# Scan of a hybrid transformer block: decay exponents as whole products with strictly triangular matrices, rows on ScalarE, weights on VectorE, prepared during the rotation

## The reference, cut to what matters

```
a_cum = jnp.cumsum(dt_c * a, axis=2)                       # within a chunk of 128 tokens
seg = a_cum[:, :, :, None, :] - a_cum[:, :, None, :, :]    # i minus j, per head
decay = jnp.exp(jnp.where(lower, seg, -jnp.inf))
scores = jnp.einsum('bcihn,bcjhn->bcijh', c_c, b_c) * decay * dt_c[:, :, None, :, :]
y_diag = jnp.einsum('bcijh,bcjhp->bcihp', scores, x_c)
y_off = jnp.einsum('bcihn,bchpn,bcih->bcihp', c_c, h_in, jnp.exp(a_cum))
```

## Time and profile before

| | us |
|---|---|
| median of 3 runs (lowest, highest) | 1417.57 (1416.66, 1420.8) |
| span of the profiled execution | 1417.9 |
| TensorE busy | 1172.4 (83%) |
| VectorE busy | 463.5 (33%) |
| ScalarE busy | 266.9 (19%) |
| GpSimd busy | 122.1 (9%) |

### The profile page before, as it was taken

The page is one execution under the profiler, slowest core; times in us unless marked ns, Lnnn a source line. Parts: engine busy times, 40 slices in busy tenths (PEclk is TensorE's granted clock), DMA queues, the critical chain, the costliest instruction groups (busy, mean ns, idle before and its releaser), DMA issues.

```text
span 1417.9 us, 15930 instructions
## 1 busy us (share of the span) xinstructions
PE 1172.4 (83%) x6032; PEld 567.1 (40%) x6032; DVE 463.5 (33%) x1121; ACT 266.9 (19%) x592; POOL 122.1 (9%) x107
## 2 busy tenths in 40 slices
PE   5899978878989599999985499986799699995553
PEld 2363433444654333333332447432468333332222
DVE  5111456764742611111101421357663511110003
ACT  1220101223530411111101322001251311110002
POOL 2000031820000010000000200033200100000001
PEclk9999999979899799999998699997689799997776
DMA  9622106739996389999999401006003689999972
GB/s 337 242 86 93 60 0 261 289 131 412 374 353 274 140 326 372 389 390 395 395 399 397 187 4 56 0 0 237 0 1 119 252 313 385 388 410 413 407 327 93
DMA packets 86997, 344.03 MB, mean 243 GB/s; under 512 B 6918, under 2 KB 42187, under 8 KB 64395
## 3 DMA queue, kind: packets, MB, share of 16 engines
q1 hardware_dynamic: 67728, 309.68, 56.5%
q10 hardware_dynamic: 15195, 19.86, 4.1%
q0 software_dynamic: 4000, 13.49, 2.7%
HBM read 300.92 MB, written 42.07 MB: 242 GB/s over the span
## 4 chain that ended last, share of the span: by engine, by line
PE 61%; DMA 20%; DVE 11%; ACT 3%; issue 2%; SPq 1%; POOL 1%; ACTq 0%; POOLq 0%; DVEq 0%
PE ps L901 13%; PE ps L503 12%; DMA ring<-in_exp_w_up 10%; PE ps L924 6%; PE ps L791 6%; PE ps L512 5%; PE ps L446 4%; DMA ring<-in_w_mod 3%; DMA slots<-arena 2%; PE ps L468 2%; DMA arena<-in_exp_w_up 2%; PE ps L688 2%; PE ps L770 2%; PE ps L668 2%; PE ps L740 1%
## 5 line engine op out<-in xcount | busy, mean ns | idle before, releaser
L901 PE MATMUL ps<-ring,arena 128*32 128x256 f32 (+1 forms) x1344 | 197.8, 534 | 45.1 <-DMA ring<-in_exp_w_up 45.1
L503 PE MATMUL ps<-u,ring 128*128 128x512 f32 (+1 forms) x416 | 168.0, 564 | 9.5 <-ACT u L1743 4.0
L446 PE MATMUL ps<-cst,arena 128*128 128x128 f32 x558 | 110.3, 318 | 65.7 <-DVE arena L1445 33.0
L446 PEld LDWEIGHTS ps<-cst,arena 128*128 128x128 f32 x558 | 70.2, 160 | 172.0 <-issue 81.5
L901 PEld LDWEIGHTS ps<-ring,arena 128*32 128x32 f32 (+1 forms) x1344 | 71.3, 136 | 154.4 <-issue 146.5
L1601 DVE TENSOR_TENSOR arena<-arena,ps 128x128 f32<-128x128 f32 (+1 forms) x59 | 27.3, 503 | 317.3 <-ACT arena L1903 317.3
L503 PEld LDWEIGHTS ps<-u,ring 128*128 128x128 f32 x416 | 80.0, 194 | 94.9 <-issue 90.1
L901 PE MATMUL ps<-arena 128*64 128x512 f32 (+1 forms) x544 | 82.2, 528 | 17.6 <-DMA arena<-in_exp_w_up 17.6
L924 PE MATMUL ps<-arena 128*32 128x256 f32 (+1 forms) x672 | 94.4, 485 | 1.6 <-ACT arena L1912 1.6
L791 PE MATMUL ps<-u,ring 128*128 128x512 f32 (+1 forms) x256 | 83.6, 487 | 2.3 <-DVE h L1426 1.3
L512 PE MATMUL ps<-ring,u 128*128 128x256 f32 (+1 forms) x224 | 76.6, 502 | 7.7 <-DVE arena L1245 7.7
(11 more groups left out here) (291 smaller groups left out, 1221.9 us busy)
## 6 DMA issues: line engine op xcount, KB each, us to landing
ring<-in_w_mod SPq DMA_DIRECT2D x24, 2048.0 KB, 10.9
ring<-in_exp_w_gate SPq DMA_DIRECT2D x22, 2048.0 KB, 18.6
ring<-in_exp_w_up SPq DMA_DIRECT2D x22, 2048.0 KB, 23.0
arena<-in_exp_w_down SPq DMA_DIRECT2D x22, 2048.0 KB, 20.1
slots<-zeros SPq DMA_DIRECT2D x4, 6144.0 KB, 41.9
arena<-in_exp_w_gate SPq DMA_DIRECT2D x10, 2048.0 KB, 20.7
u<-in_exp_w_down SPq DMA_DIRECT2D x10, 2048.0 KB, 19.7
arena<-in_exp_w_up SPq DMA_DIRECT2D x10, 2048.0 KB, 26.7
```

The costliest lines, as they stand in the source:

```text
L446: return nc.tensor.transpose(dst, src, ident[0:n, 0:n])
L503: last = nc.tensor.matmul(bank[row:row + width, 0:T - c0], w[:, k, n:n + width], u[:, k, c0:T], start=(k == 0), stop=(k == KT - 1))
L901: last = nc.tensor.matmul(ps[n * part:n * part + n, 2 + b % 2, 0:2 * width].rearrange("p (s n) -> p s n", s=2), x_k, pair[:, :, a:a + widt ...
```

## The change

Column i of head h of `rows` keeps its content, but the matrix that it is multiplied with is now strictly triangular. With M the strict triangle, (M^T rows) at (j, i) is the sum of dt*a over the tokens k with j < k <= i (forwards), which is the whole exponent. Where j is not before i the sum is empty and gives 0. So the subtraction of the sum at j and the clamp are gone, and ScalarE's exp reads the two PSUM banks itself. The masked scores, which are 0 outside the triangle, stay. The two strict matrices are made by VectorE at the end of `latents_up`, in each layer, into ground of `wuq`.

Placement: `rows` are made by ScalarE, eight instructions each, instead of one on GpSimd. `weights` is one 128x1024 product on VectorE instead of two of 128x512 on GpSimd. For tile 0 the scores, both casts, both exponentials and both weights stand in the rotation; for tile 1 the scores, casts and exponentials do, and its weights come in the scan. In the scan both casts of tile i+2 are made after the y sums of tile i. The modulation parts of layer 0 move behind the y sums (one, then two); their number is the same.

```
-SCAN_MODS = (1, 1, 1)
+SCAN_MODS = ((1, 2), (0, 0))
+        strict = [wuq[:, 0, P * d:P * d + P] for d in range(2)]
 TensorE, rotate(l):
+                masked_products(l, 0)
+                cast_rows(l, 0, 0)
                 for m in range(4):
-                    if m == 2 and l == 0:
-                        project_z(l, TT - 1)
+                    if m == 2:
+                        cast_rows(l, 0, 1)
+                        if l == 0:
+                            project_z(l, TT - 1)
...
                     spare(1)
+                masked_products(l, 1)
+                for d in range(2):
+                    cast_rows(l, 1, d)
                 read_back(f"kr{l}")
 cast_rows:
+                if n == 0:
+                    pe.wait_ge(S("to_end_ready"), l + 1)
                 pe.wait_ge(S("rows_built"), 2 * tiles_before(l) + n + 1)
                 if n >= 1:
-                    pe.wait_ge(S("decay_clamped"), 2 * tiles_before(l) + n)
+                    pe.wait_ge(S("decay_exp"), 2 * tiles_before(l) + n)
                 for b in range(2):
-                    last = nc.tensor.matmul(ps[:, 2 + b, :], ones[:, :],
+                    last = nc.tensor.matmul(ps[:, 2 + b, :], strict[d],
 TensorE, scan_tiles(l), after the y sums of tile i:
                     if i + 1 < len(tiles):
-                        cast_rows(i + 1, 1)
-                        spare(SCAN_MODS[1])
+                        spare(SCAN_MODS[l][0])
                     if i + 2 < len(tiles):
-                        scores(i + 2)
-                        cast_rows(i + 2, 0)
-                        spare(SCAN_MODS[2])
+                        masked_products(l, i + 2)
+                        cast_rows(l, i + 2, 0)
+                        spare(SCAN_MODS[l][1])
+                        cast_rows(l, i + 2, 1)
 VectorE, latents_up(l), at its end:
+                for d in range(2):
+                    link(tt(strict[d], tri[1 - d], ident, ALU.subtract))
 VectorE, rotate(l):
+                masked_scores(l, 0)
                 for m in range(4):
...
+                weights(l, 0, 0)
                 for hh in range(DA_H):
...
+                masked_scores(l, 1)
+                weights(l, 0, 1)
 VectorE:
+            def weights(l, i, d):
+                dve.wait_ge(S("decay_exp"), 2 * tiles_before(l) + 2 * i + d + 1)
+                own_read()
+                part = ews[i % 2][d].rearrange("p (g h) i -> p g h i", g=2)
+                tt(part, part, gms[i % 2][:, d].unsqueeze(2).to_broadcast([P, 2, 4, P]), ALU.mult).then_inc(
+                    S("w_ready"), 1)
 VectorE, scan_tiles(l):
                     if i + 1 < len(tiles):
-                        clamp(i + 1, 1)
+                        for d in range(2):
+                            weights(l, i + 1, d)
 ScalarE, scan(l):
+                def rows(i, d):
+                    at_dt = 32 * d + 8 * (FIRST_T[l] + i)
+                    for hh in range(SSD_H):
+                        last = a(ews[i % 2][d][:, hh, :], tri[d], ACT.Identity, scale=sc[:, 2, at_dt + hh:at_dt + hh + 1])
+                    last.then_inc(S("rows_built"), 1)
+
+                def decays(i, d):
+                    act.wait_ge(S("rows_cast"), 2 * tiles_before(l) + 2 * i + d + 1)
+                    a(ews[i % 2][d], ps[:, 2:4, :].rearrange("p b (h i) -> p (b h) i", i=P), ACT.Exp).then_inc(
+                        S("decay_exp"), 1)
+
+                act.wait_ge(S("to_end_ready"), l + 1)
+                for d in range(2):
+                    rows(0, d)
+                for d in range(2):
+                    decays(0, d)
                 wait_evac(f"z{l}{TT - 1}")
+                for d in range(2):
+                    rows(1, d)
                 a(z[:, FIRST_T[l]:TT, :], z[:, FIRST_T[l]:TT, :], ACT.Silu).then_inc(S("z_ready"), 1)
                 exp_and_ln()
+                for d in range(2):
+                    decays(1, d)
                 for i in range(n):
-                    if i + 1 < n:
-                        decays(i + 1, 1)
+                    if i + 2 < n:
+                        act.wait_ge(S("y_summed"), tiles_before(l) + i + 1)
+                        for d in range(2):
+                            rows(i + 2, d)
                     act.wait_ge(S("y_gated"), tiles_before(l) + i + 1)
...
                     if i + 2 < n:
-                        decays(i + 2, 0)
+                        for d in range(2):
+                            decays(i + 2, d)
```

More of the change, by code:

```diff
@@ L649, in scan_states, with masked_products, cast_rows @@
                         project_z(l, z_after(l, n))
+            def masked_products(l, i):
+                t = FIRST_T[l] + i
+                for g in range(2):
+                    bank = open_bank(f"cb{l}{t}{g}")
+                    r = slice(64 * g, 64 * g + 64)
+                    close_bank(nc.tensor.matmul(bank[:, 0:P], xbc[r, 4, P * t:P * t + P],
+                                                xbc[r, 5, P * t:P * t + P], start=True, stop=True))
+            def cast_rows(l, i, d):
+                n = 2 * i + d
+                if n == 0:
+                    pe.wait_ge(S("to_end_ready"), l + 1)
+                pe.wait_ge(S("rows_built"), 2 * tiles_before(l) + n + 1)
+                if n >= 1:
+                    pe.wait_ge(S("decay_exp"), 2 * tiles_before(l) + n)
+                for b in range(2):
+                    last = nc.tensor.matmul(ps[:, 2 + b, :], strict[d],
+                                            ews[i % 2][d][:, 4 * b:4 * b + 4, :].rearrange("p h i -> p (h i)"),
+                                            start=True, stop=True)
+                last.then_inc(S("rows_cast"), 1)
@@ L673, in scan_tiles @@
-                scores(0)
-                for d in range(2):
-                    cast_rows(0, d)
-                    spare(SCAN_MODS[0])
-                scores(1)
-                cast_rows(1, 0)
                 for i, t in enumerate(tiles):
@@ L2046, in skip @@
                                     xb(bcast[:, l, B_D:B_D + 8]), ALU.mult).then_inc(S("skip_ready"), 1)
-                def weights(i, d):
-                    pool.wait_ge(evacuated, entry[f"cb{l}{tiles[i]}1"] + 1)
-                    pool.wait_ge(S("decay_exp"), 2 * tiles_before(l) + 2 * i + d + 1)
-                    for gg in range(2):
-                        part = ews[i % 2][d][:, 4 * gg:4 * gg + 4, :]
-                        last = g.tensor_tensor(part, part, gms[i % 2][:, d, gg, :].unsqueeze(1).to_broadcast(
-                            [P, 4, P]), ALU.mult)
-                    last.then_inc(S("w_ready"), 1)
-                rows(0, 0)
-                rows(0, 1)
                 pool.wait_ge(filled, entry[f"state{l}{len(state_steps(l)) - 1}"] + 1)
@@ L2062, in _ @@
                 skip(0)
-                pool.wait_ge(filled, max(entry[f"z{l}{t}"] for t in tiles) + 1)
-                rows(1, 0)
-                rows(1, 1)
-                weights(0, 0)
-                weights(0, 1)
                 x_dt(1, 0)
-                weights(1, 0)
                 for i in range(len(tiles) - 1):
@@ L2074, in _ @@
                     if i + 2 < len(tiles):
-                        rows(i + 2, 0)
-                        rows(i + 2, 1)
-                    weights(i + 1, 1)
-                    if i + 2 < len(tiles):
                         x_dt(i + 2, 0)
@@ L2082, in _ @@
                     skip(i + 1)
-                    if i + 2 < len(tiles):
-                        weights(i + 2, 0)
                 experts(l)
```

61 lines of the change are left out of this document (9 added, 52 removed).

## The result

The changed kernel takes 1401.2 us at the median (1399.74 to 1403.86, 4 runs) where the kernel before, on the same chip, takes 1417.92 (1416.66 to 1420.8, 4 runs): a ratio of 0.9874, 95% interval 0.9855 to 0.9894. Timed a second time, beside other kernels, it took 1403.78 for 1421.19, a ratio of 0.9887 (0.9867 to 0.9908). The forecast of 1398.6 holds within its range. The profiled run took 1400.99 us with a span of 1399.2, 18.7 less than the span in the earlier trace rows; the medians differ by 16.7.

What follows compares the result with a forecast made beforehand. TensorE, busy 83% of the span, was taken as the bound, with its waits and half clock to win. Gains of 11.0 us in layer 0 and 8.0 in layer 1 took 1417.6 to 1398.6 us, range 1389 to 1412.

Steps and rivals of the forecast that it cites:

- Layer 0's stage, 11.0 won: Layer 0, third z projection to last y sums: 85.3 us become 73.7, less 0.56 for the strict matrices, 11.0 won.
- 10 to 12: Sign to look for in layer 0: the last y sums end 10 to 12 us earlier.
- Layer 1's stage, 8.0 won: Layer 1's rotation and scan: last y sums end at 1003.6 to 1004.2, before at 1012.15; about 8.0 us won.
- VectorE's products held up by GpSimd's rows: Layer 1's rotation: slowed VectorE products, 3.3 us, called the largest single piece of that layer's gain.
- Strict matrices 0.56 a layer: Ahead of the scan's states: two linked VectorE products of 0.28 us each, on the path, 0.56 us lost per layer.
- Everything behind shifts: Attention, router and expert weights behind the scans move earlier as a whole, so the stages' gain goes through.
- The rival in which it eats layer 0's gain: Attention's modulation weight copies (16.18 us of DMA) leave only layer 1's 8 us: 1409.6; within a partial-gain chance of 0.20.
- Nothing lies around the span: Whole kernel: span 1417.9 and runs' median 1417.57 differ by 0.3 us, so nothing of size lies outside the span.
- The sum: Whole kernel: 11.0 plus 8.0 is 19.0 us won, taken from 1417.6 for 1398.6 us.
- the clock holds too: Rival: full clock also in layer 1's last y sums (3.6 us) and layer 0's first attention steps (2.1): 1392.9; chance 0.12.
- The slower rival: Hand-overs in the rotation keep TensorE at half clock until the y sums, 27 us added: 1425.6; chance 0.09.
- ScalarE behind a table load: ScalarE before tile 1's exponential: a 1.38 us drain behind each load would cost 0.6 us over both layers; not summed.

Runs made afterwards that it cites:

- formula_only: The kernel before with only the new exponents (strict matrices, no clamp); rows and weights stay on GpSimd, all in the scan: 1398.31 us, ratio 0.9852.
- strict_hidden: The changed kernel with the strict matrices made behind the memsets of the states: 1401.02 us, ratio 0.9884.
- fill: The changed kernel plus unread products, two ahead of layer 1's second y sums and two ahead of each attention's last y transposes: 1395.51 us, ratio 0.9844.
- late: The changed kernel with scores, casts and weights of tiles 0 and 1 put back to the start of the scan: 1436.44 us, ratio 1.0119.
- formula_best: The kernel before with the new exponents, strict matrices made behind the memsets, and two unread products ahead of each attention's last y transposes: 1398.02 us, ratio 0.9878.
- late_reordered: As late, but on ScalarE tile 1's rows, silu and the two table loads stand before the first exponential: 1406.39 us, ratio 0.9915.

## Why the prediction was right, point by point

- **Layer 0's stage, 11.0 won.** From the z projection's end 85.3 became 74.7 where 73.7 was worked out, and the whole stage won 9.6. Since 2.6 us were lost before the first state product, the last sums end only 7.0 us earlier in the trace's own time, not 10 to 12. The unit costs held: cast 1.91, rows 2.4 us (2.45 forecast), weight 1.23 (1.22), exponential's hand-over to the next cast 1.21 (1.15), the modulation row's wait 0.98 (1.0), the y banks' 0.40 (0.3), ScalarE's waits at most 1.21, clock 1.00 from 216 to 291. Not forecast: the state products ahead of the stage ran at half clock (8 in 2.08 us at 184.74 behind a wait of 2.74), about 1 us.
- **Layer 1's stage, 8.0 won.** 77.4 became 69.6, so 7.8. The wait for the y banks was 3.11 for a forecast of 2.9, the sums of the last tile 9.6 (from 984.80 to 994.4) for 8.7. The step that failed is the one that put the gain down to a cause: "VectorE's products held up by GpSimd's rows (3.3 us) are the largest single piece". formula_only keeps rows and hold-ups (two products of the rotation take 2.10 and 2.00 us from 950.37 on), and its stage is 68.4. What the clamp cost was priced as a duration between two casts; that it also kept the reading of the y banks back, 4.1 us, the prediction did not see, though the wait of 4.89 was in its rows.
- **Strict matrices 0.56 a layer.** 0.61 measured; in layer 0 on the path up to the first state product, 0.3 to 0.6 of it still there at the last sums (strict_hidden). Layer 1 doesn't show it.
- **Everything behind shifts.** Attention took 108.7 and 61.0 us where it took 108.7 and 60.9; the modulation copy moved by 7.07 us and kept its length. The rival in which it eats layer 0's gain fell.
- **Nothing lies around the span.** It does: the runs take about 1.8 us more than their span (1400.99 and 1399.2; up to 2.8 in fill). The sum starts from the median of the runs, which holds these 1.8 us before and after, so they are no part of the miss of 2.6. What they tell is that the profiled execution before, at a span of 1417.9, was some 2 us slower than the median one: span against span 18.7 us were won, median against median 16.7, for a forecast of 19.0.
- **The sum.** The 18.7 us of span are layer 0's stage 9.6, layer 1's 7.8, and 2.9 between the layers and 1.1 at the end, in unchanged code, less 2.6 lost before the first state product and 0.1 in attention. The stages won 17.4 where 19.0 was forecast. The pieces in unchanged code are within its scatter, so that the span's 18.7 stands so near the 19.0 is in part luck.
- **The rival "the clock holds too" (1392.9)** did not come in this kernel. fill shows that its price was right in kind: half of the last sums at full clock and a stage 2.0 us shorter, against 3.6 that the rival set for all of them.
- **The slower rival**, half clock through the rotation, did not come: in layer 0's rotation no wait is over 1.21 and the clock is 1.00. In layer 1's TensorE waits up to 2.14 us for VectorE, and two of its four casts run at half clock (3.45 us at 953.37, 3.78 at 969.08). late shows what the rival priced: with waits of 3.0 and 4.5 us ahead of them the casts of layer 0 take 3.51 and 3.75 us, and the kernel is slower than before. But the reason set against it, that falls come behind waits of 2.45 us and more, does not hold: in formula_only the clock falls near 984, where no wait in the 12 us before is over 0.93.
- **ScalarE behind a table load.** The prediction weighed a drain of 1.38 us from the Trainium skill, "ScalarE: Activation LUTs", section "What ACT_TABLE_LOAD costs". Silu starts 1.30 us after its load (238.18 and 239.48), 0.02 behind its end: no drain here, and the measurement decides.

The stage's arithmetic was right, and the reading of what the change is made of was not. The question that the prediction left out is what the formula would do alone, and the answer is: 1394.7 to 1398.3, no worse than the whole and in the timing side by side better. The cast that the change takes out from between the sums of layer 1 was what TensorE did while VectorE read the y banks.

## What to carry to other kernels

Price an instruction that you remove not only by its duration but by what stands behind it in its engine's order: the clamp's 2.15 us held a reading back by 4.1. Before work is pulled ahead of a wait, ask what then fills that wait: TensorE stood idle for 3.1 us where it had a cast, the sums behind ran wholly at half clock, and the stage was 1.2 to 1.4 us longer than with the formula alone. And time each part of a compound change alone, on the same chip and by the stages it touches, since the part may beat the whole.

## What the hardware showed that was not expected

- Half clock can cost most in code that nobody changed. After layer 1's last sums the granted clock stays at 0.50 for about 30 us in the changed kernel and about 21 in formula_only, in two profiles of each, and attention takes 61.0 and 61.1 against 56.7 twice. In strict_hidden, with the changed kernel's wait, it is about 26, and attention takes 58.9. TensorE is 100% busy for the last 14 us before the return in the changed kernel (1010.2 to 1024.5), all at 0.50.
- Unread products in a wait of 3.1 us kept half of the next sums at full clock in fill (2.00 us for 3.67). The attention of formula_best, which has such products too, lost 6.5 us, but late_reordered has that length without them. What decides when the clock falls and when it returns was not settled.
- Unchanged code varies by 4.7 us between the layers and 3.9 before the first state product, with a granted clock of 0.77 to 0.94 in the first 60 us.
